# Other start offsets, within 256 bytes of a partition, for the projection's token blocks and the experts' split weights

## What is computed

```
conf_u, q, k, v, af, ab, r, sc_u = split(h @ w_in)
y   = concat([conformer_conv(conf_u), gla_output(o_lat, r), short_conv(sc_u)]) @ w_out
x   = x + m2 * y
h   = modulate(rmsnorm(x, norm2_w), m3, m4)
for each expert e: xs = h[idx[e]]
    hid = silu(xs @ w1[e]) * (xs @ w3[e]);  y[idx[e]] += (hid @ w2[e]) * gate[e]
out = rmsnorm(x + m5 * y)
```

## Time and profile before

| | us |
|---|---|
| median of 3 runs | 2160.54 |
| lowest and highest | 2156.77, 2160.68 |
| the profiled execution's own time | 2161.86 |
| its span, first to last instruction | 2160.2 |
| TensorE (PE) busy, weight loads (PEld) | 2058.5, 1799.7 |
| VectorE (DVE), ScalarE (ACT) busy | 1370.1, 996.1 |
| mean granted TensorE clock, share of full | 0.983 |

### The profile page before, as it was taken

One profiled execution on the slowest core, in us unless ns is written; L12 is line 12 of the kernel. 1 busy time (PEld: TensorE's weight loads), 2 busy tenths in 40 slices (PEclk: granted clock), 3 DMA queues, 4 the chain that ended last, 5 costly groups with the idle time before them and its releaser, 6 DMA issues.

```text
span 2160.2 us, 34796 instructions
## 1 busy us (share of the span) xinstructions
PE 2058.5 (95%) x13421; PEld 1799.7 (83%) x13421; DVE 1370.1 (63%) x2082; ACT 996.1 (46%) x1631; POOL 278.3 (13%) x357
## 2 busy tenths in 40 slices
PE   6999999999999899995799999999999999999996
PEld 4778888778877677783799999999999999999985
DVE  3664648995994577757555655566565665556557
ACT  5923454344531445432444544444444444445455
POOL 0000000000001010020011122111221212111120
PEclk9999999999999899998899999999999999999998
DMA  7463333332427665456357656576565765667565
GB/s 257 150 250 128 108 106 99 119 118 80 125 83 233 234 208 179 143 212 255 118 184 265 214 194 220 188 272 206 179 226 206 265 196 187 217 224 247 200 234 224
DMA packets 188285, 407.93 MB, mean 189 GB/s; under 512 B 15957, under 2 KB 53397, under 8 KB 187301
## 3 DMA queue, kind: packets, MB, share of 16 engines
q1 hardware_dynamic: 162212, 318.36, 42.8%
q0 software_dynamic: 25984, 88.39, 12.6%
HBM read 329.59 MB, written 77.12 MB: 188 GB/s over the span
## 4 chain that ended last, share of the span: by engine, by line
PE 78%; DVE 11%; DMA 4%; ACT 3%; issue 3%; SPq 2%; POOL 0%; DVEq 0%; ACTq 0%; POOLq 0%
PE bh L55 11%; PE bh L56 11%; PE bh L57 11%; PE bank L55 8%; PE bank L57 8%; PE bank L56 8%; PE eby L55 5%; PE eby L57 5%; PE eby L56 5%; DVE acc L848 4%; DMA wraw<-in_w_in_dram 1%; PE ebt L2271 1%; PE bank L1025 1%; DVE over L2000 1%; PE bank L1407 1%
## 5 line engine op out<-in xcount | busy, mean ns | idle before, releaser
L55 PE MATMUL bh<-xt_hi,shi 128*128 128x256 f32 x2048 | 572.8, 280 | 4.2 <-DVE slo L2420 2.7
L56 PE MATMUL bh<-xt_lo,shi 128*128 128x256 f32 x2048 | 572.1, 279 | 0.0
L57 PE MATMUL bh<-xt_hi,slo 128*128 128x256 f32 x2048 | 571.9, 279 | 0.0
L2420 DVE TENSOR_TENSOR slo<-raw,shi 128x1024 fp32r<-128x1024 f32 x384 | 456.1, 1222 | 156.5 <-ACT shi L2329 151.9
L2329 ACT ACTIVATE shi<-raw 128x1024 fp32r<-128x1024 f32 x384 | 389.8, 1052 | 127.1 <-PE eby L57 125.5
L55 PEld LDWEIGHTS bh<-xt_hi,shi 128*128 128x128 f32 x2048 | 386.0, 188 | 5.5 <-issue 2.5
L56 PEld LDWEIGHTS bh<-xt_lo,shi 128*128 128x128 f32 x2048 | 386.2, 189 | 0.6
L57 PEld LDWEIGHTS bh<-xt_hi,slo 128*128 128x128 f32 x2048 | 386.1, 189 | 0.0
L55 PE MATMUL bank<-h_hi,whi 128*128 128x512 f32 x704 | 283.0, 402 | 1.2 <-DVE wlo L711 1.2
L57 PE MATMUL bank<-h_hi,wlo 128*128 128x512 f32 x704 | 275.5, 391 | 0.0
L56 PE MATMUL bank<-h_lo,whi 128*128 128x512 f32 x704 | 275.3, 391 | 0.0
(11 more groups left out here) (344 smaller groups left out, 3086.6 us busy)
## 6 DMA issues: line engine op xcount, KB each, us to landing
raw<-in_exp_w_dram SPq DMA_DIRECT2D x96, 2048.0 KB, 11.1
uT<-stage POOLq DMA_DIRECT2D x72, 256.0 KB, 2.7
xb<-in_ada_w_dram SPq DMA_DIRECT2D x24, 512.0 KB, 5.5
wraw<-in_w_in_dram SPq DMA_DIRECT2D x22, 512.0 KB, 5.1
adaw<-in_ada_w_dram SPq DMA_DIRECT2D x8, 1024.0 KB, 9.9
xb<-in_x_dram SPq DMA_DIRECT2D x16, 512.0 KB, 4.4
xt<-in_x_dram POOLq DMA_DIRECT2D x16, 512.0 KB, 5.3
x2d<-xt POOLq DMA_DIRECT2D x16, 512.0 KB, 3.4
```

Of the source, the lines that this page charges most:

```text
L55: nc.tensor.matmul(out, w_hi, x_hi, start=start, stop=False)
L56: nc.tensor.matmul(out, w_hi, x_lo, start=False, stop=False)
L57: return nc.tensor.matmul(out, w_lo, x_hi, start=False, stop=stop)
L2420: nc.vector.tensor_tensor(item_dst(slo, n), item_src(n), item_dst(shi, n), ALU.subtract).then_inc(S["w_lo_ready"], 1)
```

## The change

The tensors `h_hi` and `h_lo` become flat, 32 words (128 bytes) longer, and `blocks` cuts four blocks out of each, shifted by 4, 8, 16 and 24 words. Modulo 256 the blocks of `h_hi` then begin at 16, 32, 64 and 96 and those of `h_lo` at 144, 160, 192 and 224. `area` adds 128 bytes for part 1, so `wo_lo`, `wo_raw`, `cat1`, `srf`, `scuf`, `mb` and `h2t` move to 128, while `wo_hi`, `ct_hi` and `ct_lo` stay at 0. In the experts 32 bytes follow each split buffer: `shi0` to `shi3` begin at 0, 32, 64 and 96, `slo0` to `slo3` at 128, 160, 192 and 224; `xt_*` stay at 32 and `ht_*` at 0. All that is allocated behind moves by 256 bytes and keeps its offset. To make room, `msq`, 18 words used in the first stage's root, moves into the tile `tok`, which is not yet used then.

```diff
--- before.py
+++ after.py
@@ -238,7 +238,8 @@
         small = v.pair_decay[:, :, :].rearrange("p h c -> p (h c)")
         st1, st2 = small[:, 0:16], small[:, 16:32]
         modt = small[:, 32:64].rearrange("p (s j) -> p s j", s=2)
-        ssq, msq, rst = (sb(n, [P, 18]) for n in ("ssq", "msq", "rst"))
+        ssq, rst = (sb(n, [P, 18]) for n in ("ssq", "rst"))
+        msq = v.tok[:, :, :].rearrange("p e s -> p (e s)")[:, 0:18]
         bank, (zb, bvk, bu, bsf, bsb) = v.bank[0:NBANK], v.bank[NBANK:8]
         tpb = [zb, bvk, bu, bsf]
         S = {n: sem("b_" + n) for n in (
@@ -307,7 +308,7 @@
             if g == 0:
                 return lambda t, k: t[:, k, :]
             n, c = divmod(g - 1, 2)
-            return lambda t, k: t[:, n, k, c * 2 * P:(c + 1) * 2 * P]
+            return lambda t, k: t[n][:, k, c * 2 * P:(c + 1) * 2 * P]
 
         def by_row(ap):
             return ap.rearrange("(r p) -> r p", p=P)
@@ -983,7 +984,7 @@
                         pe.wait_ge(S["act_read"], act_reads(u - NBANK))
                 w = area(n)[2]
                 w_hi, w_lo = weights_of(i)
-                x_hi, x_lo = (v.hc_hi, v.hc_lo) if n == 4 else (v.h_hi[:, n, :, :], v.h_lo[:, n, :, :])
+                x_hi, x_lo = (v.hc_hi, v.hc_lo) if n == 4 else (v.h_hi[n], v.h_lo[n])
                 for k in range(KD):
                     if u < NEARLY and i == 0:
                         pe.wait_ge(S["h_lo_ready"], k + 1 + (0 if n == 4 else KD * (2 * n + 2)))
@@ -1115,7 +1116,7 @@
 
         def area(n, part):
 
-            return place(low + (4 * part + n) * AREA)[0]
+            return place(low + (4 * part + n) * AREA + part * SHIFTS * 4)[0]
 
         cat = [area(0, i)(f"cat{i}", [P, KD, NB]) for i in range(2)]
         take = area(0, 1)
@@ -2111,8 +2112,11 @@
             return tile
 
         raw, raw_loaded = v.raw, v.s_raw
-        shi = [sb(f"shi{i}", [P, D], F32R) for i in range(NR)]
-        slo = [sb(f"slo{i}", [P, D], F32R) for i in range(NR)]
+        shi, slo = [], []
+        for n, half in (("shi", shi), ("slo", slo)):
+            for i in range(NR):
+                half.append(sb(f"{n}{i}", [P, D], F32R))
+                at[0] += 32
         xs_words = [sb(f"xs{i}", [P, D], F32R) for i in range(2)]
         xs = [t[:, :].bitcast(F32) for t in xs_words]
         at[0] += 32
@@ -2544,6 +2548,15 @@
                 loop(dve, body)
 
 
+SHIFTS = 32
+
+
+def blocks(tile):
+
+    places = [n * KD * NB + shift for n, shift in enumerate((4, 8, 16, 24))]
+    return [tile[:, o:o + KD * NB].rearrange("p (k c) -> p k c", k=KD) for o in places]
+
+
 def trunk_kernel(nc, v):
 
     in_use = []
@@ -2570,7 +2583,7 @@
         with nc.Block() as block:
             with ExitStack() as hst:
                 hsb, ps = alloc(nc, hst)
-                v.h_hi, v.h_lo = hsb("h_hi", [P, L // NB, KD, NB], F32R), hsb("h_lo", [P, L // NB, KD, NB], F32R)
+                v.h_hi, v.h_lo = (blocks(hsb(n, [P, L // NB * KD * NB + SHIFTS], F32R)) for n in ("h_hi", "h_lo"))
                 high = nc.sbuf_base
                 v.bank = [ps(f"bank{i}", [P, 512]) for i in range(8)]
                 with ExitStack() as cst:
```

## The result

The changed kernel takes 2182.5 us (median of 4 runs, 2181.34 to 2183.96) against 2160.61 of the kernel before (4 runs): a ratio of 1.0102 with a 95% interval of 1.009 to 1.0114. It is slower by 22 us, where 6 us faster was forecast, and lies outside the range. The profiled execution took 2182.5 us.

A forecast was written before the change was run, and what follows sets the result against it. TensorE's matmul pace was taken to bound the kernel, fully in the experts and partly before. Terms -4.4 - 0.8 - 4.3 + 3.4 = -6.1 us gave 2154.4 us against the median of 2160.54, range 2142 to 2167.

The forecast's parts named there:

- offsets do nothing: Rival, whole kernel: the 3.3 ns between paces came from other work running then; time 2160.5 us, chance 0.17.
- the price: All matmuls: 3.3 ns (120.0 less 116.7) gained wherever a distance leaves 0, lost where it becomes 0.
- distance 0 is the only bad one: All matmuls: load and stream starting at the same place modulo 256 meet once more, one extra stall of 3.3 ns.
- Item 1: Projection, L55 to L57: 2112 matmuls leave distance 0, 7.0 us of TensorE's time, 4.4 us gained on the chain.
- Item 2: Output projection: only L56, moving `wo_lo`, leaves distance 0 (to 128), 256 matmuls, 0.8 us gained.
- share of 0.62: Projection: part of the matmuls' time on the chain, 321 of about 520 us, the rest hidden behind convolution and DMA waits.
- Item 3: Experts, down: 1280 of 3 x 512 matmuls gain 3.3 ns, 4.3 us; buffer 0's L55 and L57 stay at distance 0.
- Item 4: Experts, up: buffer 1 falls to distance 0, 1024 matmuls lose 3.4 us; the other 5120 taken as unchanged.
- Items 5 and 6: Splits on ACT and DVE, and DMA into moved tiles: both taken as costing nothing, DMA possibly 0 to 3 us.
- the convolution did not take over: Rival, projection: DVE's convolution chain hides all of its gain, sum -1.7 us, 2158.8 us, chance 0.08.
- The slower rival: Up products lose a step at 5120 matmuls, 17.1 us; net +15.5, 2176 us; chance 0.18 including half-way to it.
- The faster rival: All stages: wider distances save a second step, 29 us in all, 2131 us; chance 0.17 including half-way to it.

The follow-up runs named there:

- paces: Microbenchmark, matmuls alone, 120 per set of offsets, no other engine at work: at distance 0, 226.7 ns with 512 columns and 120.0 ns with 256.
- proj_only: The changed kernel with the experts' split buffers back at offset 0: 2170.63 us against 2159.65 for the kernel before, ratio 1.0048.
- experts_only: The kernel before with only the experts' split buffers shifted and `msq` moved into `tok`: 2173.0 us against 2159.65, ratio 1.0052.
- xt_112: The kernel before with only `xt_*` moved, as one tile, from offset 32 to 112: 2140.55 us against 2158.97, ratio 0.991.
- xt_64: The kernel before with only `xt_*` moved from offset 32 to 64: 2167.26 us against 2160.91, ratio 1.003.
- all_at_32: The kernel before with split buffers and `ht_*` at 32 and `xt_*` at 96, keeping a distance of 64: 2167.7 us against 2160.91, ratio 1.0029.
- slo_128: The kernel before with `msq` in `tok` and all four `slo` at offset 128, `shi` at 0: 2179.09 us against 2159.65, ratio 1.0089.

## Why the prediction was wrong

**What bounds the kernel** held: TensorE's pace sets the time, and an offset within 256 bytes changes it. That offsets do nothing, the rival with a chance of 0.17, is refuted by the slower time and by `paces`. The Trainium skill, "TensorE: Matmul & The Clock Gate", Part 2, says that a weight load takes nothing from the running matmul. The runs do not show which of the two is held up, but they speak against it: with the moving operand left where it was (offset 0, 512 columns), moving the stationary one from 0 to 32 took `paces` from 226.7 to 233.3 ns. Over all distances 256 columns took 113.3 to 121.8 ns and 512 columns 226.7 to 238.

**The step that failed** is the price: "3.3 ns ... taken as gained wherever a distance leaves 0". It was read from 256 columns (the earlier trace rows against the earlier trace rows) and laid on matmuls of 512 columns, of which the trace had distance 0 only. The reading that gave it, "distance 0 is the only bad one", was wrong in its sign for 512 columns: there nothing measured is better than distance 0, and what leaves it loses 2 to 8 ns at the multiples of 32. That 512 columns cost 13.3 ns over their columns as 256 do at distance 0 was taken for one common cause; `paces` shows it is no sign that 512 columns had anything to give back. From one offset of a size nothing follows for another offset of that size.

By items:

- Item 1, projection, forecast -4.4. The windows give 231.9 ns in the mean over the four blocks, 2112 x 5.2 = +11 us of TensorE's time. They are steady stretches; the mean of the whole group rose by 4 ns only (402 to 406), which gives 2112 x 4 = +8 us.
- Item 2, output projection, forecast -0.8 and "only L56". All three lines slowed. 22 matmuls in the kernel before and the 22 that answer to them in the kernel after:

```profile
887.55:892.55 5.00, 5.00 (x23) 1.00 0.43 147
```

```profile
886.48:891.62 5.14, 5.14 (x23) 1.00 0.36 123
```

  227.3 against 233.6 ns for a mean over L55, L56 and L57. One operand out of step takes the other two lines with it. By the mean of the group (397 to 401) item 2 is 768 x 4 = 3 us, by this window 4.8. Items 1 and 2 together were timed by `proj_only` at +10.4 (7.3 to 13.2). That is two thirds of the 16 us of the windows and nearly all of the 11 of the group means, so the share of 0.62 on the chain is not confirmed. It is no constant either: on the chain of 52:700 the products L55 to L57 hold 58.1% in the kernel after (49.6% before) and the convolution 11.2% (13.6% before).
- Item 3, down, forecast -4.3. 231.4 ns over buffers 0 to 2 against 226.7: 1536 x 4.7 = some +7 us. Buffer 0's L55 and L57 stood at distance 0 still and slowed with the rest: in the mean over its later item (f = 4) of 14 experts the next start follows L55 after 230.3 ns, L56 after 228.7 and L57 after 232.9, all 226.6 to 226.8 before.
- Item 4, up, forecast +3.4 with all of it at buffer 1 and 120 ns there. Measured +0.43 us on each 384, 16 x 0.43 = +6.9, at buffers 0, 1 and 2, and a gain at buffer 3. The mean was mis-sized by a factor of two within its bounds, and its distribution was wrong. Items 3 and 4 together were timed by `experts_only` at +11.2 (7.8 to 14.7), the sum of the windows being 14; the stretch of the experts in the traces grew by 14.2 us there and by 13.2 in the kernel after (1095.7 to 1108.9).
- Items 5 and 6, nothing for the splits and the DMA, held, and the convolution did not take over.

The slower rival had a chance of 0.18 and a time of 2176, but its mechanism, only +32 clears the meeting and others act like 0, is wrong too: it has no loss at 512 columns. The faster rival's 113.3 ns exists for full loads with 256 columns, which `xt_112` turned into 18.4 us, but not through this change.

Neither of the signs that the prediction named for being wrong occurred: the projection did not stay at 226.7 ns, and up did not show 120 at buffers 2 and 3. Neither of them was a loss at 512 columns, which is what came.

**What stays open**: why the paces are what they are. No rule found here gives the pace from the offsets, nor from the stream ahead, and none of the runs separates the weight load's reads from the moving operand's.

## What to carry to other kernels

Where TensorE's stream is the bound and each matmul has its own weight load, the start of both operands modulo 256 bytes is a size to be measured: with fp32r and 512 columns keep all operands at the same offset; with 256 columns measure the pair in the order and behind the stream that the kernel has. A price per matmul read at one number of columns must not be laid on another. A microbenchmark of twenty lines, with no other engine at work, gave the sign and the size at 512 columns; at 256 columns and distance 64 it promised 113.3 ns where the kernel ran at 117.8, until the kernel's own stream was put ahead. A layout can be worth 1% either way without an instruction added or removed.

## What the runs showed of the hardware

- The pace of a stream of fp32r matmuls with a load of 128 columns each depends on the distance of the operands' starts modulo 256: 113.3 to 121.8 ns for 256 columns, 226.7 to 238 for 512, at a granted clock of 1.00.
- Adding the same offset to all operands changed nothing where it was tried behind the same stream or at distance 0 (226.7 ns with 512 columns and all at 0, 32 and 128; `xt_64` and `all_at_32` within 0.5 us).
- Three products that share operands slow down together: with one of the four tiles out of step the mean over all three rises (`slo_128`, down 226.7 to 233.3 ns, +0.89% of the kernel; the output projection 227.3 to 233.6 ns).
- A stream can have several steady paces at one distance, and which it takes changes with the stream ahead: at 64, 113.3 or 117.8 ns with 256 columns and 229.0 or 233.3 with 512, held to the end of the 72 matmuls.
- The length of the load matters too: with 256 columns at distance 0, 113.3 ns over 32 stationary columns and 120.0 over 128; with 512 columns 231.7 and 226.7.
